# First layer's small transfers on two DMA queues: parameter rows between weight units, log steps and narrow columns issued by ScalarE

## What is computed

```
for l in range(2):
    h = rmsnorm(x, norm_mix[l])
    x = x + mixer(h, w_in[l], ...)        # h @ w_in: q, k, v, gates of four branches
    x = x + cross_attention(rmsnorm(x, norm_xattn[l]), rmsnorm(mem, norm_mem[l]), ...)
    h = rmsnorm(x, norm_mlp[l])
    x = x + square(relu(h @ w1)) @ w2
return rmsnorm(x, norm_final)
```

## Time and profile before

| what | value |
|---|---|
| median of 3 runs | 1950.54 us (1949.77 to 2742.4) |
| the profiled execution | 1949.91 us |
| its span, first to last instruction | 1948.1 us |
| granted clock of PE, mean | 0.999 |
| busy in the span | PE 1931.3, VectorE 1249.7, GpSimd 1127.9, ScalarE 961.8 us |
| DMA | 191.41 MB, mean 98 GB/s |

### The profile page before, as it was taken

One profiled execution on the slowest core, in us unless ns is written; L12 is line 12 of the kernel. 1 busy time (PEld: TensorE's weight loads), 2 busy tenths in 40 slices (PEclk: granted clock), 3 DMA queues, 4 the chain that ended last, 5 costly groups with the idle time before them and its releaser, 6 DMA issues.

```text
span 1948.1 us, 33275 instructions
## 1 busy us (share of the span) xinstructions
PE 1931.3 (99%) x12707; PEld 1641.5 (84%) x12707; DVE 1249.7 (64%) x1909; ACT 961.8 (49%) x1665; POOL 1127.9 (58%) x1356
## 2 busy tenths in 40 slices
PE   7999999999999999999999999999999999999998
PEld 6788788888888889999887887888898888999997
DVE  5888778856145766767358786787641556667661
ACT  6754645345445644444456647353554655344334
POOL 4565564956834555766565555467576355566653
PEclk9999999999999999999999999999999999999999
DMA  6423233333422333333342233333343233333332
GB/s 187 119 73 85 82 83 88 87 109 107 148 82 81 99 99 102 99 103 98 98 102 79 72 87 82 81 83 87 120 130 124 66 98 95 111 104 98 103 98 81
DMA packets 196091, 191.41 MB, mean 98 GB/s; under 512 B 23834, under 2 KB 186204, under 8 KB 195548
## 3 DMA queue, kind: packets, MB, share of 16 engines
q1 hardware_dynamic: 194780, 187.19, 32.7%
q10 hardware_dynamic: 1152, 2.10, 0.3%
HBM read 185.04 MB, written 3.15 MB: 97 GB/s over the span
## 4 chain that ended last, share of the span: by engine, by line
PE 95%; ACT 2%; DVE 2%; DMA 1%; issue 0%; SPq 0%; POOL 0%; DVEq 0%; ACTq 0%
PE gemm L701 73%; PE mix L701 20%; DMA w_raw<-in_w_in_dram 1%; DVE work L1974 0%; DVE work L1965 0%; PE mix L1283 0%; DMA work<-in_norm_mix_dram 0%; DVE sums_raw L1965 0%; PE mix L944 0%; PE mix L1178 0%; ACT w_hi L1429 0%; ACT work L1819 0%; DMA w_raw<-in_mlp_w_dram 0%; PE mix L877 0%; ACT work_split L1579 0%
## 5 line engine op out<-in xcount | busy, mean ns | idle before, releaser
L694 POOL TENSOR_TENSOR w_lo<-w_raw,w_hi 128x256 fp32r<-128x256 f32 x676 | 584.8, 865 | 793.0 <-ACT w_hi L1429 793.0
L695 POOL TENSOR_TENSOR w_lo<-w_raw,w_hi 128x256 fp32r<-128x256 f32 x676 | 595.8, 881 | 0.0
L701 PE MATMUL gemm<-h_hi,w_hi 128*128 128x512 f32 x1248 | 493.7, 396 | 0.5 <-DVE h_lo L1974 0.5
L701 PE MATMUL gemm<-h_lo,w_hi 128*128 128x512 f32 x1248 | 486.2, 390 | 0.0
L701 PE MATMUL gemm<-h_hi,w_lo 128*128 128x512 f32 x1248 | 486.1, 390 | 0.0
L701 PE MATMUL gemm<-work_split,w_hi 128*128 128x512 f32 (+1 forms) x1552 | 446.9, 373 | 0.3
L1429 ACT ACTIVATE w_hi<-w_raw 128x512 fp32r<-128x512 f32 x676 | 380.0, 622 | 62.8 <-DMA w_raw<-in_w_in_dram 24.6
L701 PEld LDWEIGHTS gemm<-work_split,w_hi 128*128 128x128 f32 x1552 | 281.6, 189 | 51.0 <-DVE work_split L1974 1.1
L701 PE MATMUL gemm<-work_split,w_lo 128*128 128x512 f32 (+1 forms) x776 | 288.5, 372 | 0.0
L701 PEld LDWEIGHTS gemm<-h_hi,w_hi 128*128 128x128 f32 x1248 | 234.3, 188 | 56.7 <-issue 6.6
L701 PEld LDWEIGHTS gemm<-h_hi,w_lo 128*128 128x128 f32 x1248 | 234.3, 188 | 49.5
(11 more groups left out here) (372 smaller groups left out, 2792.9 us busy)
## 6 DMA issues: line engine op xcount, KB each, us to landing
w_raw<-in_mlp_w_dram SPq DMA_DIRECT2D x256, 256.0 KB, 2.7
w_raw<-in_w_in_dram SPq DMA_DIRECT2D x208, 256.0 KB, 2.7
w_raw<-in_xattn_w_kv_dram SPq DMA_DIRECT2D x64, 256.0 KB, 3.0
w_raw<-in_w_branch_dram SPq DMA_DIRECT2D x32, 256.0 KB, 2.7
w_raw<-in_w_out_dram SPq DMA_DIRECT2D x32, 256.0 KB, 2.7
w_raw<-in_xattn_w_q_dram SPq DMA_DIRECT2D x32, 256.0 KB, 2.8
w_raw<-in_xattn_w_o_dram SPq DMA_DIRECT2D x32, 256.0 KB, 2.7
w_raw<-in_w_in_dram SPq DMA_DIRECT2D x32, 128.0 KB, 3.5
```

Of the source, the lines that this page charges most:

```text
L694: pool.tensor_tensor(lo[:, 0:half], raw[:, 0:half], hi[:, 0:half].bitcast(F32), ALU.subtract)
L695: pool.tensor_tensor(lo[:, half:], raw[:, half:], hi[:, half:].bitcast(F32), ALU.subtract).then_inc(split_ready, 1)
L701: return pe.matmul(o, w, a, start=start, stop=stop, skip_group_check=True)
```

## The change

- `param_rows` no longer issues the two log step transfers of a layer.
- The two halves of x behind unit 0 come behind unit 1.
- Mem and the masks no longer follow unit 8. Layer 0's 19 rows are issued five at a time after units 8, 9, 10 and 11 (four after the last), mem after unit 11. The masks follow unit 25 and are counted on `p_dma` (`pro_loads`), for which VectorE waits before its first `pick`.
- Layer 1's rows go two at a time after units 15 to 24, where before three went after each of units 13 to 21.
- GLA's matrix and S5's b and c follow unit 26 instead of unit 14 in layer 0.
- ScalarE issues the four log step transfers (both layers) and layer 0's two narrow ones, behind its split of unit 7 and ahead of its first `h_hi`; then it splits units 8 and 9, of which unit 9 came after the first values before.
- The counts that PE and ScalarE wait for on `p_rows` are 22 instead of 23.

```diff
--- before.py
+++ after.py
@@ -541,12 +541,6 @@
 
             def param_rows(l, landed):
                 stage = Rf(24 + l, 1)[:, 0:P]
-                for a in range(2):
-
-                    src = s5_log_step[l].rearrange("(t a) -> a t", a=2)[a:a + 1, :]
-                    sp.dma_start(SM[64 * a:64 * a + 64, 16 + 8 * l:24 + 8 * l],
-                                 src.to_broadcast([64, 8]), allow_slow_non_contiguous=True).then_inc(landed, 16)
-                    yield
                 for name, src in (("norm_mix", norm_mix), ("norm_xattn", norm_xattn), ("norm_mem", norm_mem),
                                   ("norm_mlp", norm_mlp), ("mlstm_conv_b", mlstm_conv_b), ("mlstm_norm", mlstm_norm),
                                   ("gla_norm", gla_norm), ("hgrn_norm", hgrn_norm), ("gla_b_a", gla_b_a),
@@ -627,8 +621,8 @@
                     else:
                         sp.dma_start(WR[:, u % RING, :].rearrange("p (k c) -> p k c", k=2),
                                      src.rearrange("(k p) c -> p k c", p=P)).then_inc(raw_in[u % RING], 16)
-                    if u == 12 or (L < DEPTH - 1 and (name, part) == ("up1_0", 0)):
-                        nl = L if u == 12 else L + 1
+                    if L < DEPTH - 1 and (name, part) == ("up1_0", 0):
+                        nl = L + 1
                         for what, wide, to in (("m_i", 8, 0), ("g_a", RANK, 8)):
                             src = w_in[nl][:, COL[what]:COL[what] + wide].rearrange("(k p) c -> p k c", p=P)
                             sp.dma_start(NW[:, :, to:to + wide], src, allow_slow_non_contiguous=True).then_inc(nw_in, 16)
@@ -636,27 +630,30 @@
                         for half in range(2):
                             src = norm_final[half * 512:half * 512 + 512].rearrange("(a b) -> a b", a=1)
                             sp.dma_start(GAINS[half], src.to_broadcast([P, 512])).then_inc(nw_in, 16)
-                    if u == 0:
+                    if u == 1:
                         for t in (0, 2):
                             sp.dma_start(Rf(2 * t + 1, 1), x[0, t * P:(t + 1) * P, 512:]).then_inc(p_x2, 16)
                     if u == 4:
                         sp.dma_start(CO[:, P:], consts[:, P:]).then_inc(p_dma, 16)
                     if u == 8:
+                        sp.wait_ge(p_pe, 1)
+                        rows0, rows1 = param_rows(0, p_rows), param_rows(1, p_x[1])
+                    if 8 <= u < 12:
+                        for _ in range(5):
+                            next(rows0, None)
+                    if u == 11:
                         sp.dma_start(R(20, 4).rearrange("p (t a) b -> p t (a b)", t=2),
                                      mem[0].rearrange("(t p) d -> p t d", p=P)).then_inc(p_rows, 16)
-                        sp.dma_start(LM[:, :, :], level_masks.rearrange("p (l c) -> p l c", c=CH)).then_inc(p_rows, 16)
-                        sp.wait_ge(p_pe, 1)
-                        for _ in param_rows(0, p_rows):
-                            pass
-                        rows1 = param_rows(1, p_x[1])
                         sp.wait_ge(p_pe, 7)
-                    if 13 <= u < 22:
-                        for _ in range(3):
+                    if 15 <= u < 25:
+                        for _ in range(2):
                             next(rows1, None)
+                    if u == 25:
+                        sp.dma_start(LM[:, :, :], level_masks.rearrange("p (l c) -> p l c", c=CH)).then_inc(p_dma, 16)
                     if u == UNIT["gate3_0"]:
                         sp.wait_ge(p_act, 3)
                         sp.dma_start(mem_scratch, YR[:, 0:4, :].rearrange("p a b -> p (a b)")).then_inc(p_out, 16)
-                    if unit == (14 if L == 0 else 10):
+                    if unit == (26 if L == 0 else 10):
                         if L:
                             sp.wait_ge(ss["kk_done"], L * PER_LAYER["s5_kk_done"])
                         else:
@@ -945,7 +942,7 @@
                 return i
 
             def params(l):
-                pe.wait_ge(p_x[1] if l else p_rows, 16 * 22 if l else 16 * 23)
+                pe.wait_ge(p_x[1] if l else p_rows, 16 * 22)
                 pe.transpose(M[3 - l][:, 0:P], Rf(24 + l, 1)[:, 0:P], ident).then_inc(p_pe, 1)
 
             def mem_columns():
@@ -1609,6 +1606,17 @@
                 now[0] = L
                 th_n[0] = 0
                 factors(0)
+                if L == 0:
+                    feed(first_unit("r_i") + 8)
+                    for l, landed in ((0, p_rows), (1, p_x[1])):
+                        for a in range(2):
+                            src = s5_log_step[l].rearrange("(t a) -> a t", a=2)[a:a + 1, :]
+                            act.dma_start(SM[64 * a:64 * a + 64, 16 + 8 * l:24 + 8 * l],
+                                          src.to_broadcast([64, 8]), allow_slow_non_contiguous=True).then_inc(landed, 16)
+                    for what, wide, to in (("m_i", 8, 0), ("g_a", RANK, 8)):
+                        src = w_in[0][:, COL[what]:COL[what] + wide].rearrange("(k p) c -> p k c", p=P)
+                        act.dma_start(NW[:, :, to:to + wide], src, allow_slow_non_contiguous=True).then_inc(nw_in, 16)
+                    feed(first_unit("r_i") + 10)
                 first = 6 if L else 2
                 norm_hi(0, first)
                 values_out("r_i")
@@ -1616,7 +1624,7 @@
                 values_out("g_v")
                 norm_hi(6, 8)
                 if L == 0:
-                    act.wait_ge(p_rows, 16 * 23)
+                    act.wait_ge(p_rows, 16 * 22)
                     for t in range(2):
                         do(act.activation(flat(R(16, 2)), flat(R(20 + 2 * t, 2)), ACT.Square, accum_out=SM[:, 40 + t:41 + t]))
                     do(act.activation(SM[:, 42:44], SM[:, 40:42], ACT.Ln, scale=1.0 / D, bias=eps))
@@ -2214,6 +2222,8 @@
                         stt(PTA[:, 1, PROW[name]:PROW[name] + 2], PS[:, 22 + n, 0:2], 0.0, PS[:, 20 + n, 0:2], ALU.min, ALU.subtract)
                 pr = lambda n: PS[:, n, :]
                 re_, im_ = PTA[:, now[0], PROW["s5_lam_re"]:PROW["s5_lam_re"] + 8], PTA[:, now[0], PROW["s5_lam_im"]:PROW["s5_lam_im"] + 8]
+                if L == 0:
+                    dve.wait_ge(p_dma, 32)
                 pick(hg, 0)
 
                 if L == 0:
```

## The result

The changed kernel takes 1960.23 us (median of 4 runs, 1959.51 to 1961.89), the kernel before 1950.22 us on the same chip: ratio 1.0054, 95% interval [1.0038, 1.007]. It is 10 us slower, outside the range of the prediction. The profiled execution took 1959.51 us with a span of 1957.7 us, 9.6 us above that of before.

The account below looks back on a forecast made before the run. PE bounds the kernel, busy 99% of the span. 1949.91 − 0.70 − 0.39 + 0.6 = 1949.4 us, plus 0.4 for the way to the median, gave 1949.8 us, range 1948.5 to 1953.0.

Parts of the forecast that it names:

- What bounded the kernel: PE, busy 99% of the span at full clock; transfer edits can only touch its few remaining waits.
- the two prices: PE time to be regained: 0.70 us at the `h_lo` wait near 46.7, 0.39 us at `params_all` near 80.
- unit 14 was late through elements: Weight unit 14 took 10.62 us to land because 4-byte log step elements stood ahead of it on SyncE's queue.
- The new wait at 37.73: PE's transpose of layer 0's parameters waits for log steps now issued at 25.8: 0.6 us, bounds 0 and 3.2.
- The parts costed at nothing: Moving rows, mem, masks, GLA and S5 loads and x's second halves costs PE nothing, all landing before they are wanted.
- the two old waits: PE's waits on `h_lo` and `params_all` both go, since unit 14 would land by 38.
- the paragraph on ScalarE's six issues: Six transfers issued at about 25.8 us take 4.1 to 6.3 us of ScalarE; cost to PE nothing, bounds 0 to 0.5.
- the very next paragraph: Layer 0's log steps now gate PE at 37.73; a pair takes 7.6 to 11.1 us after its first issue.
- Rival B: SyncE's weight units 12 to 14 held behind ScalarE's elements; PE loses 3 to 5 us: 1953 us, chance 0.10.
- Rival A: Layer 0's log steps land late and gate PE at 37.73, +1.2 to +7 us: typically 1952 us, chance 0.25.

Follow-up runs that it names:

- run 3: Changed kernel with each layer's log steps as one 64-byte piece to each of 128 partitions, still issued by ScalarE; 1949.33 us, ratio 0.9995.
- run 4: Kernel before with only the log steps turned into 64-byte pieces, one transfer a layer on SyncE's queue; 1949.29 us, ratio 0.9996.
- run 5: Changed kernel's order, but 64-byte log steps and narrow columns all on SyncE, ScalarE issuing nothing; 1948.78 us, ratio 0.9994.
- run 6: Changed kernel with layer 0's log steps as 64-byte pieces, layer 1's still 4-byte elements, all on ScalarE; 1948.57 us, ratio 0.9993.
- run 1: Changed kernel with layer 1's two log step transfers back on SyncE, layer 0's and the narrow ones left on ScalarE; 1952.12 us, ratio 1.001.
- run 8: Changed kernel with the narrow columns on SyncE behind unit 20, all four element log step transfers left on ScalarE; 1957.12 us, ratio 1.0035.
- run 2: Changed kernel with all four log step transfers back on SyncE, ScalarE issuing only the narrow columns; 1950.15 us, ratio 1.0001.
- run 7: Changed kernel with layer 1's log steps and the narrow columns issued by ScalarE only behind its last h_hi; 1957.45 us, when repeated 1952.35 us.

## Why the prediction was wrong

**Right.** What bounded the kernel, and the two prices: −0.70 us was −0.8 and −0.39 was −0.4, −1.2 together in runs 3 to 6. That unit 14 was late through elements (run 4). The new wait at 37.73: forecast 0.6, measured 0.9 as idle time and 1.05 as a shift, 1.0 and 0.7 in runs 1 and 8. The parts costed at nothing (rows, mem, masks, S5's and GLA's loads, x's halves): run 5 has the whole order and none of the waits at issue.

**Right by luck.** That the two old waits are gone in the changed kernel itself. The forecast wanted unit 14 to land by 38, and within 6 us of its issue; it landed at 49.5, after 17.4 us. PE came to its old waiting place 10 us late, at 57.48 instead of 47.42, and so did not meet the lateness. Unit 14 in time, and the waits gone with it, is what runs 3 to 5 show (2.6 to 2.8 us to land).

**The step that failed** is the paragraph on ScalarE's six issues: "I take nothing for it, with 0 to 0.5 us as bounds". Its upper end took one held issue, of the length that SyncE's had once in the rows of before (to 33.4). But before, two element transfers stood in the queue when that row was held; here four did, with two more issues behind them. The time that they take was in the text's own rows: the 2 us windows at 0.05 and 0 GB/s. Worked out from these, a pair of transfers takes the "7.6 to 11.1 us after its first issue" that the very next paragraph uses for the landing; two pairs take twice that, from 26 to between 41 and 48, and an issue behind them waits for most of it. Rival B in the same text does count "some 20 us of elements"; at 109 a microsecond the 2048 elements take 18.8. The same elements were thus counted for their own landing and not for the engine that issues behind them. I had the term at 0 to 0.5; it measured 7.8, and the half clock that followed the wait, for which the sum had no term, 2.2 more.

**Rival B** was right in kind (units in the other queue are held) and had the wrong weight: 0.10, against the argument that "the elements keep an engine busy 5% of the time". Run 8 shows that this argument is void. In the 9 us from 29 to 38 SyncE's queue had units 12 to 14 to bring and passed 118 packets, all before 31 and none of them a weight unit's (they are the rest of mem), beside 941 elements. Low share of the DMA engines was the mark of the trouble, and I took it as room. Its price of 3 to 5 us was right for PE's waits (4.9 in run 8); it left out the half clock behind them (2.0). Rival A's 7 us had the right size by a mechanism that didn't occur: PE was held by layer 0's log steps for 1.05 us in the changed kernel, and no more than 1.3 in any run.

The Trainium skill's sentence cited in the prediction (DMA: Bandwidth & Descriptors, "Issuing engines are not separate DMA queues") told the direction: run 8 agrees that the engine that issues gives no path of its own. The same section says that the sequencer's time to issue is usually small relative to the transfer itself. That doesn't hold here: the sixth issue was held 8.82 us of the 18.1 us until its transfer had landed, and the six together took 18.3. The same page's "Queues, rings and completion order" says that each DMA engine goes round the queues packet by packet. By that alone unit 12 should have passed among the elements at once; run 8 measured 19.0 us for it, with none of its packets before 39 us. The measurement decides, and what makes the element traffic of one queue hold the other is not settled by these runs.

**What I can't tell apart.** Runs 3 and 4 changed the size of the pieces (64 for 4 bytes) and their number (128 for 1024 a layer) at once; which of the two counts was not tried. No run issues all four element transfers on SyncE at some 25 us, so whether the 10 us come from ScalarE's queue or from 2048 elements at once at that place is not set apart either; in run 2 the two pairs stand in two places. Nor was it tried to avoid the half clock with the wait left in. Runs 3 to 6 are 1.0 to 1.7 us under their runs of before, all with intervals that include no change, so none is shown to be faster; the profiles alone show the waits gone, 1.2 us of PE's time in each.

## What to carry to other kernels

Price a transfer by its pieces, and find the pace in the trace (here 109 four-byte elements per us at a DMA share of 0.05, so that 2 KB cost 4.7 us); a share near zero while something waits is not free room. Moving such a transfer to the queue of a compute engine moves its hold onto that engine's own instructions and still holds the other queue: give each issue behind it the whole backlog as the upper bound of its price, and compare that with the engine's next due time (here 35.4 us). The better cure here was to load small vectors in contiguous pieces and to pick from them on an engine with time to spare (VectorE, two small copies a layer).

## What the runs showed of the hardware that I had not expected

- Elements in one queue hold up the other one's transfers: beside four element transfers a 256 KB unit took 14.2 to 21.1 us (changed kernel and run 8, units 12 to 15) where it takes 2.7, while the DMA engines stood at 0.05 for long stretches.
- An issue is held although few are outstanding: the fourth, fifth and sixth of ScalarE's took 4.28, 3.02 and 8.82 us in the changed kernel. In run 8 the same four element issues took 0.70 us each; why the fourth is held in one kernel and not in the other no run shows. In run 2 the two narrow ones took 1.02 us together.
- The 2048 narrow pieces of 32 and 64 bytes are much faster than as many elements: in run 3 both narrow transfers had landed 7.4 and 8.9 us after their issue, with 2368 packets of ScalarE's queue between 24 and 37 us, beside 2.1 MB of SyncE's.
- A wait of 7.5 us cost 2.2 us more, at a granted clock of 0.5, and in run 8 two waits of 2.2 and 2.3 us, with 2.3 us of products between them, cost 2.0 more in the same way; waits of 0.9 to 1.3 us in runs 1 and 7 were followed by no such stretch.
